# Hybrid decoder layer on one core: routing done per token tile, and expert rows gathered through an index table

## What is computed

```python
h = h + hybrid_mixer(hn, ...)            # ends in merged @ w_out
hn = rmsnorm(h, norm_ffn[l])
h = h + hier_moe(hn, ...)
...
glog = (xt @ w_group) + b_group                       # (T, 4)
gsel = jnp.argmax(glog, axis=-1)
gw = take_along_axis(softmax(glog), gsel)
elog = ((xt @ w_expert) + b_expert).reshape(T, 4, 8)
ev, ei = lax.top_k(elog[gsel], 2)
ew = jax.nn.softmax(ev, axis=-1) * gw
eid = gsel * 8 + ei
...
y = (jax.nn.silu(xb @ w1[e]) * (xb @ w3[e])) @ w2[e]  # rows xb of the tokens of expert e
out = segment_sum(y * buf_w, buf_tok)
```

## Time and profile before

| | us |
|---|---|
| median of three runs (lowest to highest) | 1778.69 (1776.9 to 1779.84) |
| profiled execution, its own time | 1784.23 |
| its span, first to last instruction | 1782.4 |
| PE busy in it | 1557.8 (87%) |
| DVE, ACT, POOL busy in it | 537.1 (30%), 348.3 (20%), 262.8 (15%) |
| mean granted TensorE clock | 0.954 of full speed |
| HBM read and written | 276.06 MB, 57.41 MB |

### The profile page before, as it was taken

How to read it: one execution, slowest core, us unless ns; L and a number is a source line. 1 busy time by engine, 2 the same in 40 slices (tenths; PEclk the granted TensorE clock), 3 DMA queues, 4 the chain that set the end, 5 groups by cost and what they waited for, 6 DMA issues and landing times.

```text
span 1782.4 us, 20856 instructions
## 1 busy us (share of the span) xinstructions
PE 1557.8 (87%) x7526; PEld 828.0 (46%) x7527; DVE 537.1 (30%) x1378; ACT 348.3 (20%) x859; POOL 262.8 (15%) x363
## 2 busy tenths in 40 slices
PE   6999998989989898988999994199799999889990
PEld 3554543434444444443444552156355666446650
DVE  4210005665565545553222215011011111101116
ACT  3000003343433433342000111011011111111112
POOL 2000002333232232221000000300000000000003
PEclk9999999999999999998999997599899999999995
DMA  9124602443111111002536410979999999999967
GB/s 254 26 59 57 132 0 100 166 142 95 30 33 34 30 24 42 25 18 77 204 115 232 172 53 18 341 283 380 383 389 384 379 391 381 391 390 383 381 223 283
DMA packets 130215, 334.21 MB, mean 188 GB/s; under 512 B 36792, under 2 KB 72664, under 8 KB 120944
## 3 DMA queue, kind: packets, MB, share of 16 engines
q1 hardware_dynamic: 112208, 291.88, 46.8%
q0 software_dynamic: 9552, 29.55, 5.0%
q10 hardware_dynamic: 8400, 12.07, 1.9%
HBM read 276.06 MB, written 57.41 MB: 187 GB/s over the span
## 4 chain that ended last, share of the span: by engine, by line
PE 71%; DMA 9%; DVE 8%; SPq 6%; issue 3%; ACT 2%; POOL 2%; ACTq 0%; POOLq 0%; DVEq 0%
PE PS L741 13%; PE PS L642 10%; PE PS L531 10%; PE PS L755 7%; PE PS L704 6%; PE PS L673 5%; SPq L301 5%; PE PS L628 4%; PE PS L589 4%; PE PS L608 3%; PE PS L526 2%; DMA BA<-w 2%; DMA WA<-w 2%; DMA BA<-rows_d 2%; DVE mx L1022 1%
## 5 line engine op out<-in xcount | busy, mean ns | idle before, releaser
L642 PE MATMUL PS<-WA 128*128 128x512 f32 x512 | 260.3, 621 | 17.8 <-ACT WA L833 17.8
L741 PE MATMUL PS<-WA,BA 128*64 128x256 f32 x2048 | 235.8, 388 | 14.1 <-DMA WA<-w 12.9
L741 PEld LDWEIGHTS PS<-WA,BA 128*64 128x64 f32 x2048 | 172.9, 140 | 84.6 <-issue 22.1
L531 PE MATMUL PS<-WA,BA 128*128 128x512 f32 x416 | 183.1, 601 | 5.1 <-DVE WA L937 5.1
L1248 POOL TENSOR_SCALAR BA<-BA,rin,gates 128x640 f32<-128x640 f32 (+7 forms) x128 | 99.8, 780 | 301.8 <-DVE rin L1045 301.7
L1161 DVE SCALAR_TENSOR_TENSOR BA<-BA,PS 128x256 f32<-128x256 f32 x46 | 19.4, 421 | 408.4 <-ACT BA L880 408.4
L642 PEld LDWEIGHTS PS<-WA 128*128 128x128 f32 x512 | 85.6, 191 | 111.5 <-issue 80.9
L826 ACT ACTIVATE BA<-PS,ngm 128x640 f32<-128x640 f32 (+7 forms) x128 | 89.7, 701 | 218.2 <-DVE ngm L1023 218.0
L531 PEld LDWEIGHTS PS<-WA,BA 128*128 128x128 f32 x416 | 79.6, 193 | 103.9 <-issue 98.3
L755 PE MATMUL PS<-WA,BA 128*64 128x512 f32 x512 | 116.9, 597 | 11.7 <-DVE BA L1171 7.6
L1287 POOL DMA_DIRECT2D BA<-rows_d x92 | 48.1, 522 | 531.1 <-PE PS L722 528.1
(11 more groups left out here) (207 smaller groups left out, 1361.4 us busy)
## 6 DMA issues: line engine op xcount, KB each, us to landing
WA<-w SPq DMA_DIRECT2D x66, 2048.0 KB, 34.4
BA<-w SPq DMA_DIRECT2D x30, 2048.0 KB, 36.7
rows_d<-WA SPq DMA_DIRECT2D x7, 2048.0 KB, 7.5
BA<-rows_d POOLq DMA_DIRECT2D x94, 128.0 KB, 7.2
rows_d<-BA ACTq DMA_DIRECT2D x92, 128.0 KB, 7.8
WA<-w_in SPq DMA_DIRECT2D x16, 512.0 KB, 5.5
gates_d<-WA SPq DMA_DIRECT2D x32, 256.0 KB, 2.2
WA<-gates_d SPq DMA_DIRECT2D x8, 1024.0 KB, 6.0
```

Source lines behind the costliest of these rows:

```text
L531: mm = pe.matmul(PS[:, j % 4, :], ws[:, c % 6, k, :], hnT[:, k, 512 * h:512 * h + 512], start=(k == 0), stop=(k == KT - 1))
L642: mm = pe.matmul(PS[:, 6, :], gw[:, j, k, :], hnT[:, k, 512 * hf:512 * hf + 512], start=(k == 0), stop=(k == KT - 1))
L741: mm = pe.matmul(PS[DH * h:DH * h + DH, bank, 0:256], xT[:, k, :], w[par][:, k, 256 * h:256 * h + 256], start=(k == 0), stop=(k == KT - 1))
```

## The change

Four things are done in another way.

1. **Routing by tile.** `choose(m)` picks group and experts of tile `m` (16 operations on DVE, on 4 to 32 columns), `rank(m)` on PE counts with two bf16 matmuls of 32 columns, `place(m)` on DVE (5 operations) adds the running rows `next_row` of each expert and writes the tile's two entries `slotx_i`. All stand inside the output projection, at one to two tiles' distance; the router's matmuls of tile `i-1` now stand in the middle of the second half of tile `i`.
2. **An index table in place of rows.** `ids_d` in DRAM has 32 x 1024 entries of 64 bytes: 1024 for each expert, so that an entry's place needs no count of the other experts' blocks. POOL scatters 64-byte entries (16 integers that begin with twice the token's number) tile by tile. The normed rows themselves are stored once, in token order, to `hn_d` by SP. `ids_d` is zeroed by one 2 MB transfer on SP's queue at the start of attention.
3. **The weights of expert 2** are issued when the logits are done and `hn_d` has been stored; they no longer wait for a scatter.
4. **In the loop** POOL reads, for each block, 64 entries in two transfers of 64 single integers (one to each half of the partitions), waits for them, waits for `x_tr`, gathers 128 half rows of 2 KB by one indirect transfer, and waits until it has landed before it turns to the next block. The loop is now two loops, over experts and over an expert's blocks, and POOL reads an expert's two bounds before its blocks. Rows of a block that belong to no token are now copies of token 0's.

The diff, without definitions of tiles that have only moved:

```diff
+ENTRY = 16
...
-    rows_d = scratch("rows_d", ((MAXB + 1) * SLOTS, D))
+    rows_d = scratch("rows_d", (MAXB * SLOTS, D))
+    hn_d = scratch("hn_d", (2 * SEQ, D // 2))
+    ids_d = scratch("ids_d", (NE * SEQ, ENTRY), I32)
...
+        ids_z = ids_d.rearrange("r n -> (r n)").rearrange("(p a n) -> p a n", p=P, n=512)
+        sp.dma_start(ids_z, zeros.bitcast(I32).unsqueeze(1).to_broadcast([P, NE * SEQ * ENTRY // (P * 512), 512])) \
+            .then_inc(S["zero_done"], 16)
...
+        def store_normed(i):
+            sp.wait_ge(S["hn2_done"], i + 1)
+            sp.dma_start(hn_rows[P * i:P * i + P, :], mT[:, i, :, :].rearrange("p k n -> p (k n)")) \
+                .then_inc(S["hn_st"], 16)
...
+                store_normed(i - 1)
         sp.wait_ge(S["h2_done"], TT)
         sp.dma_start(h2_d[SEQ - P:SEQ, :], h2[:, (TT - 1) % 2, :]).then_inc(S[f"h2_st{(TT - 1) % 2}"], 16)
-        sp.wait_ge(S["scattered"], 16 * 2 * TT)
+        store_normed(TT - 1)
+        sp.wait_ge(S["log_done"], TT)
+        sp.wait_ge(S["hn_st"], 16 * TT)
         for b in range(2):
             sp.wait_ge(S[f"h2_st{b}"], 16 * TT // 2)
         load_expert(sp, 2, 2)
...
-        for i in range(TT + 1):
-            if i < TT:
-                if i >= 2:
-                    pe.wait_ge(S["h2_done"], i - 1)
-                for n in range(2):
-                    for k in range(KT):
-                        mm = pe.matmul(PS[:, 2 * (i % 2) + n, :], mT[:, i, k, :], wout[:, k, 512 * n:512 * n + 512],
-                                       start=(k == 0), stop=(k == KT - 1))
-                    if n == 0 and i >= 1:
-                        turn_normed(i - 1)
-                mm.then_inc(S["out_ps"], 1)
-            else:
+        def rank(i):
+            pe.wait_ge(S["assigned"], i + 1)
+            if i >= 1:
+                pe.wait_ge(S["slotx_done"], i)
+            pe.matmul(PS[:, 7, 0:NE], tri[:, :], assign[:, NE * i:NE * i + NE], start=True, stop=True)
+            pe.matmul(PS[:, 7, NE:2 * NE], ones[:, :], assign[:, NE * i:NE * i + NE], start=True, stop=True) \
+                .then_inc(S["route_ps"], 1)
+        def project(i, n, ks):
+            for k in ks:
+                mm = pe.matmul(PS[:, 2 * (i % 2) + n, :], mT[:, i, k, :], wout[:, k, 512 * n:512 * n + 512],
+                               start=(k == 0), stop=(k == KT - 1))
+            return mm
+        for i in range(TT):
+            if i >= 2:
+                pe.wait_ge(S["h2_done"], i - 1)
+            project(i, 0, range(KT))
+            if i >= 1:
                 turn_normed(i - 1)
+            if i >= 2:
+                rank(i - 2)
+            project(i, 1, range(KT // 2))
             if i >= 1:
                 router(i - 1)
-        pe.wait_ge(S["assigned"], 1)
-        pe.matmul(PS[:, 0, 0:256], tri[:, :], assign[:, :], start=True, stop=True)
-        pe.matmul(PS[:, 1, 0:256], ones[:, :], assign[:, :], start=True, stop=True).then_inc(S["route_ps"], 1)
+            project(i, 1, range(KT // 2, KT)).then_inc(S["out_ps"], 1)
+        turn_normed(TT - 1)
+        rank(TT - 2)
+        router(TT - 1)
+        rank(TT - 1)
...
+        pe.sem_inc(S["x_tr"], 1)
         pe.wait_ge(S["routed"], 1)
-        pe.wait_ge(S["x_blk"], 32)
+        pe.wait_ge(S["x_blk"], 16)
...
-                rows_in = pe.snap(b * 32 + 64)
+                rows_in = pe.snap(b * 16 + 32)
...
-            act.wait_ge(S["x_tr"], b + 2)
+            act.wait_ge(S["x_tr"], b + 3)
...
+        def first_of_max(out, src, best, b, rev):
+            step(dve.tensor_reduce(best, src, X, ALU.max))
+            step(dve.scalar_tensor_tensor(b, src, best, rev, ALU.is_equal, ALU.mult))
+            step(dve.tensor_reduce(c1, b, X, ALU.max))
+            return dve.tensor_scalar(out, b, c1, None, ALU.is_equal)
+        def choose(m):
+            dve.wait_ge(S["log_done"], m + 1)
+            groups4, experts = lgs[:, m, 0:NG], lgs[:, m, NG:NG + NE]
+            step(first_of_max(oh4, groups4, top[:, 0, m:m + 1], b4, rev4))
+            step(dve.tensor_scalar(m4, oh4, -NEG, NEG, ALU.mult, ALU.add))
+            step(dve.tensor_tensor(open32.rearrange("p (g e) -> p g e", g=NG), experts.rearrange("p (g e) -> p g e", g=NG),
+                                   m4.unsqueeze(2).to_broadcast([P, NG, EPG]), ALU.add))
+            step(first_of_max(onehot[:, m, 0, :], open32, top[:, 1, m:m + 1], b32, rev32))
+            step(dve.scalar_tensor_tensor(rest32, onehot[:, m, 0, :], 2 * NEG, open32, ALU.mult, ALU.add))
+            step(first_of_max(onehot[:, m, 1, :], rest32, top[:, 2, m:m + 1], b32, rev32))
+            dve.tensor_tensor(assign[:, NE * m:NE * m + NE], onehot[:, m, 0, :], onehot[:, m, 1, :], ALU.add) \
+                .then_inc(S["assigned"], 1)
+        def place(m):
+            dve.wait_ge(S["route_ps"], m + 1)
+            step(dve.tensor_tensor(row32, next_row, PS[:, 7, 0:NE], ALU.add))
+            step(dve.tensor_tensor(next_row, next_row, PS[:, 7, NE:2 * NE], ALU.add))
+            step(dve.tensor_tensor(pick, onehot[:, m, :, :], row32.unsqueeze(1).to_broadcast([P, 2, NE]), ALU.mult))
+            step(dve.tensor_reduce(slot_f[:, m, :], pick, X, ALU.add))
+            dve.tensor_copy(slotx_i[:, m, :], slot_f[:, m, :]).then_inc(S["slotx_done"], 1)
         dve.wait_ge(S["gff_in"], 16)
         dve.wait_ge(S["wr_in"], 64)
+        dve.wait_ge(S["tables"], 1)
         for i in range(TT + 1):
+            if i >= 2:
+                place(i - 2)
+            if i >= 1:
+                logits(i - 1)
+                choose(i - 1)
...
+        place(TT - 1)
+        dve.wait_ge(S["tables"], 2)
+        step(dve.tensor_tensor(cnt, next_row, first_row, ALU.subtract))
...
         dve.sem_inc(S["routed"], 1)
+        step(dve.tensor_tensor(G4[3][:, :, :], lgs[:, :, 0:NG], top[:, 0, :].unsqueeze(2).to_broadcast([P, TT, NG]), ALU.subtract))
+        dve.tensor_tensor(G8[4], top[:, 2, :], top[:, 1, :], ALU.subtract).then_inc(S["route_arg"], 1)
+        step(dve.scalar_tensor_tensor(base32, starts_f[:, 0:NE], float(SLOTS), first_row, ALU.mult, ALU.subtract))
+        step(dve.tensor_tensor(spread, onehot.rearrange("p t c n -> p (t c) n"),
+                               base32.unsqueeze(1).to_broadcast([P, 2 * TT, NE]), ALU.mult))
+        step(dve.tensor_reduce(moved, spread, X, ALU.add))
+        dve.tensor_tensor(slots_i[:, :, :].rearrange("p c t -> p t c"), moved.rearrange("p (t c) -> p t c", c=2), slot_f,
...
+        def scatter_ids(i):
+            pool.wait_ge(S["slotx_done"], i + 1)
+            for c in range(2):
+                g.indirect_dma_start(ids_d[:, :], bass.IndirectOffsetOnAxis(ap=slotx_i[:, i, c:c + 1], axis=0),
+                                     entry[:, i, :], None).then_inc(S["scattered"], 16)
+        pool.wait_ge(S["zero_done"], 16 * (ZPARTS + 1))
+        for i in range(TT - 2):
+            scatter_ids(i)
+        pool.wait_ge(S["out_ps"], TT)
         step(g.memset(upto, 1.0))
         g.affine_select(out=upto, in_=upto, compare_op=ALU.is_ge, fill=0.0, base=0,
                         pattern=[[1, NE], [-1, NE]], channel_multiplier=0).then_inc(S["tables"], 1)
+        for i in range(TT - 2, TT):
+            scatter_ids(i)
+        pool.wait_ge(S["scattered"], 16 * 2 * TT)
+        pool.wait_ge(S["hn_st"], 16 * TT)
+        pool.wait_ge(S["h2T_ps"], TT)
         pool.wait_ge(S["routed"], 1)
-        pool.wait_ge(S["zero_done"], 16 * ZPARTS)
-        pool.wait_ge(S["hn2_done"], TT)
-        for i in range(TT):
-            for c in range(2):
-                g.indirect_dma_start(rows_d[0:MAXB * SLOTS, :], bass.IndirectOffsetOnAxis(ap=slots_i[:, c, i:i + 1], axis=0),
-                                     mT[:, i, :, :].rearrange("p k n -> p (k n)"), None).then_inc(S["scattered"], 16)
-        pool.wait_ge(S["scattered"], 16 * 2 * TT)
+        def fetch_rows():
+            g.indirect_dma_start(xin[:, :], None, hn_d[:, :], bass.IndirectOffsetOnAxis(ap=ids[:, 0:1], axis=0)) \
+                .then_inc(S["x_blk"], 16)
+        with pool.Fori(0, NE) as e:
+            lo = pool.value_load(starts_i[0:1, bass.ds(e, 1)], min_val=0, max_val=MAXB)
+            hi = pool.value_load(starts_i[0:1, bass.ds(e + 1, 1)], min_val=1, max_val=MAXB)
+            with pool.Fori(lo, hi) as b:
+                row = nc.s_assert_within(pool.snap(e * SEQ + b * SLOTS - lo * SLOTS), 0, NE * SEQ - SLOTS,
+                                         skip_runtime_bounds_check_because="an expert has at most SEQ rows")
+                for n in range(2):
+                    pool.dma_start(ids[SLOTS * n:SLOTS * n + SLOTS, :], ids_d[bass.ds(row, SLOTS), n:n + 1],
+                                   allow_slow_non_contiguous=True) \
+                        .then_inc(S["ids_in"], 16)
+                pool.wait_ge(S["ids_in"], pool.snap(b * 32 + 32))
+                pool.wait_ge(S["x_tr"], pool.snap(b + 1))
+                pool.sem_inc(S["rows_due"], 1)
+                fetch_rows()
```

(40 more changed lines are left out.)

64 lines of the change are left out of this document (18 added, 46 removed).

## The result

The changed kernel takes 1834.98 us, the median of four runs (1831.19 to 1842.92), against 1779.26 for the kernel before on the same chip: 1.032 of before, with a 95% interval of 1.0284 to 1.0356. It is slower by 56 us. The forecast was 1922, in a range from 1825 to 1985: 144 us more than before, where 56 came. The time lies in the range, near its lower end; the sign and the mechanism came, but not half the size.

What follows compares the result with a forecast made beforehand. PE idling before the expert loop, and a loop with PE and DMA engines both full, were taken as the bounds. 1784.2 - 25 (earlier start) + 163 (POOL's longer index-then-rows cycle) = 1922 us, range 1825 to 1985.

Steps and rivals of the forecast that it cites:

- Rival 1: In the loop, the fetch of indices and rows stays hidden behind PE; time 1759 us, chance 9%.
- rival 2: Loop loss cancels the earlier start: cycle among weights 13.5 us, +26 against -25, time 1785 us, chance 3%.
- the signs I had named: Expected in the loop's profile: PE waits over 150 us, busy below 75%, DMA share about 0.8, indices 6 to 9 us.
- The hole: PE's idle stretch between output projection and expert loop, claimed to shrink by 25 us (20 to 30).
- The loop: The expert loop over 46 blocks, 582 us before, claimed to grow by 163 us.
- the split into two paces: Loop sum: 26.5 blocks at POOL's 19.3 us among weights, 19.5 others at PE's 12 us, together 745 us.
- The gather: Each block's indirect transfer of 128 half rows, priced at 9.0 us among weights, bounds 7.0 and 10.7.
- The indices: Each block's two transfers of 64 numbers ahead of the rows, priced at 8.0 us, bounds 6.1 and 9.8.
- 511 us of weights on the wires: Loop time with DMA engines full: 182.5 MB of weights plus some 14 MB of rows and results at 384 GB/s.
- Rival 3: Same loop chain with low bounds: cycle 15.4 us, +83, time 1842; high bounds 1971; no chance of its own.
- Rival 4: PE's clock falls as well after waits in the loop, costing 45 us over 19.5 blocks; time 1967, chance 8%.
- theory C: Experiments' alternative for the loop: PE's granted clock, falling to the lower level after waits, sets the pace; no chance given.

Runs made afterwards that it cites:

- e2: Changed kernel with the indices loaded once ahead of the loop, so every block gathers by the same list: 1725.72 us, 0.97 of before.
- e3: Changed kernel loading only 8 numbers of each partition of the weights of experts 3 to 31: 1715.86 us, one run.
- e5: Kernel before, with a pair of small index transfers loaded and waited for ahead of each block's direct rows, and their landing waited for: 1857.43 us, 1.0427 of before.
- e8: Changed kernel with each block's index pair loaded and waited for twice, one after the other: 1982.33 us, one run.
- e12: Kernel before with each block's rows fetched by one gather of 128 half rows, indices counted up by POOL: 1751.8 us, 0.9855 of before.
- e11: e2 with the pair of direct transfers in place of the gather, always of the same 64 rows: 1751.98 us, 0.9859 of before.
- e10: Changed kernel with the next block's indices as one transfer issued behind the gather, waited for one block later: 1733.19 us, 0.9747 of before.
- e1: Changed kernel with indices of an expert's first and second block asked for during the gather of the block before: 1809.4 us, 1.0164 of before.
- e9: Kernel before with each block's rows as one direct transfer to 128 partitions: 1970.22 us, 1.1063 of before.

## Why the prediction was wrong

**Right: the mechanism and its sign.** Indices and rows one behind the other make POOL's cycle longer than PE's, only while weights are on the wires. e2 (without the indices), e3 (without the weights), e5 (in the old kernel) and e8 (doubled) each show it from another side. Rival 1, hidden latency, and rival 2, that it cancels, are out. Of the signs I had named, the DMA share fell to 0.86 (I said 0.8), and the indices were slow in spite of 64 numbers, but landed in 5.5 in the median and the gather in 6.4, both under what I had named (6 to 9, and 8 to 10). PE did wait for the gather, in 28 blocks, but 83 us in all and not over 150, and stayed busy for 84% of the loop and not under 75%: here too the sign came and the size did not.

**The hole: 25 us forecast, 31.2 measured.** The last tile came at 1084.0 instead of 1086.9. From the first index issue (1112.03) to the first transposes (1118.76) were 6.7 instead of 9 and more, since the weights of expert 2, issued from 1096.16, were nearly through by then. From the last tile to the first transposes were 66.7 before and 34.7 now. Two rows of the timelines, and the window in which the first indices and rows came (DMA share 0.24, where it had been 0.99 from 1104 to 1112):

```profile
1084.02 1.23 DVE L1167 SCALAR_TENSOR_TENSOR BA<-PS,BA 128x1024 f32<-128x1024 f32 x1
```
```profile
1118.76 1.09 PE L761 MATMUL PS<-ident,BA 128*128 128x128 f32 x4 [18.54 <-DMA BA<-hn_d,ids]
```
```profile
1112.00:1119.00 7.00, 0.24 (x1) 0.27 (x2) 0.00 (x0) 0.00 (x0) 2.15 (x3) 0.50 0.24 82
```

**The loop: +163 forecast, +78.0 measured. This is the step that failed: the sum of 26.5 blocks at 19.3 us and 19.5 blocks at PE's pace. Three terms were mis-sized, and the split into two paces did not hold.**
1. *The gather, 9.0 from issue to landing; it took 6.4 (6.6 in the block shown).* I had taken it near the old pair's 9.8. I had no row for one gather in this traffic, and put the value near the upper bound. This is the largest mistake: 2.4 us in each block's cycle, and by my sum some 45 of the 85 us. About 1 us of it lies in the price itself: in loops that keep PE's pace the gather landed in 7.9 (e2) and 8.1 (e12) in the median, not in 9.0. The rest belongs to the changed kernel itself, in which the same gather lands sooner. It has fewer weights under way at a time: a load of 2 MB lands in 12.7 there, in 26.9 in e2, and in 34.9 before. That this is why the gather lands sooner is argued, not shown. The landings of the gather in e2 and e12, and of the weights in the changed kernel and in e2:

```profile
DMA to landing us min/median/max: 3.3/7.9/9.3
```
```profile
BA<-rows_d,ids POOLq DMA_INDIRECT x41, 8.1
```
```profile
WA<-w SPq DMA_DIRECT2D x60, 2048.0 KB, 12.7
```
```profile
WA<-w SPq DMA_DIRECT2D x59, 2048.0 KB, 26.9
```

2. *The indices, 8.0 from first issue to last landing; they took some 7 in the block shown, 5.5 from each one's issue in the median.* The rows I leaned on, 6.1 and 2.05 more, were of transfers with more traffic on POOL's own queue. Registers, waits and reads of bounds, 2.3 in my sum, took 3.5 (0.9 ahead of the gather, 2.6 behind it). So this term and the registers together came out right, by errors of opposite sign. The cycle was 17.06 instead of 19.3.
3. *511 us of weights on the wires.* I divided by the 384 GB/s of the loop before. With the gather the wires carry more: windows of the changed kernel show 418 where they are full. That is some 12 us.

```profile
1180.00:1270.00 90.00, 68.78 (x486) 41.33 (x482) 7.93 (x28) 8.15 (x16) 11.39 (x16) 0.92 1.01 418
```

My own two-pace sum with these numbers: 196.5 MB at 418 GB/s are 470 us, 470 / 17.06 = 27.5 blocks, 18.5 others at 12 are 222, together 692, +110 instead of +163. Measured were 660.4. The 32 us that are left are the sum's own error: it knows a block among weights, paced by POOL, and a block without them, paced by PE. But POOL waited for PE only once, so hardly any block ran at PE's pace, and of the 45 intervals between gathers 32 lie between 12.2 and 16.3 us: blocks of which a part had the wires free. From 1365 us on, for example, POOL waited in turn 3.5 us (rows), 7.0 (indices), 10.4 (rows), 2.2 (indices), 3.5 (rows) and 7.7 (indices). e8 says the same louder: 150 us for a doubled index latency where 230 to 280 had been expected. Rival 3, the chain with the low bounds, said 1842 and came near 1835, but by luck: its cycle was 15.4 and not 17.06, and it kept the 511 us and the two paces. A latency under load must not be multiplied as a constant when the change itself slows the engine that makes the load.

So the +78.0 is made of two parts of which I had foreseen one: +105.5 for the chain (660.4 against e2's 554.9) and -27.5 for the form of the transfer and what it does to the weights (554.9 against 582.4).

**Rival 4, the clock.** The granted clock did fall after the waits: four transposes 1.11 in place of 0.66, 16 matmuls 5.66 in place of 3.65, after 5.25 idle; in the loop PEclk is 0.94 against 0.98. It cost nothing that I can see, and theory C falls with it: POOL waited for PE once in the whole loop, so a slower PE could not hold up the next fetch; in the block after the one shown PE was again the one who waited (2.12 us); and in e2, where the chain is gone, the 1.00 came back by itself. So a PE that waits anyway lost nothing, as I had said, and nothing shows the 45 us that rival 4 gave to the other blocks.

## What to carry to other kernels

Before a dependent transfer is put into a loop, add up landings, not bytes, and take them from rows in the same traffic: an index of 4 bytes costs a whole latency, 5.5 us here against 1.9 on free wires. A table of indices is worth having (with the routing by tile it brought 31 us ahead of the loop; no run separates the two) when its entries are asked for a block ahead and waited for a block later; then 1835 became 1733. And where a change slows the engine that causes the traffic, the latencies fall with it, so neither the old latency nor the old bandwidth holds: bound the sum from both sides and don't take the upper end.

## What the runs showed of the hardware

- With a block's rows as one gather of 128 half rows by index the DMA engines moved 409 to 412 GB/s in the loop, with two direct transfers to 64 partitions each 384 to 386, for the same bytes and at a DMA share of 1.00 to 1.02 (e2, e12 against before, e11). Worth 1.5% of this kernel; the cause is open.
- Small transfers behind a gather on the same software queue land late: one of 128 numbers 9.0 us after its issue, itself 1 us behind that of the gather (e10); of four of 64 numbers one took up to 11.6 (e1). No run separates the place behind the gather from the traffic, which was fuller in e10 (401 GB/s) than in the changed kernel (339).
- The same gather landed in 6.4 in the median where a load of 2 MB took 12.7 (changed kernel), in 7.9 where it took 26.9 (e2), and in 3.4 without such loads (e3).
- A direct transfer whose two sides are ordered as (half, row, column) went out as 512 packets of about 500 bytes and landed in 14.6 us, twice the pair's 7.2 (e9).
